# Fixed places for five experts instead of three, with another set of capacities and another order of blocks, in the expert stage of a two-model kernel on one core

## The reference, cut to what matters here

```python
scores = sigmoid(h @ w_router)                       # 256 tokens x 64 experts
idx = top 8 of (scores + router_bias) within the 4 best of 8 groups
gate = scores[idx] / sum(scores[idx]) * 2.5
for each expert e, for the tokens that chose it:
    y = (silu(x @ w_gate[e]) * (x @ w_up[e])) @ w_down[e]     # 1024 -> 256 -> 1024
    out[token] += gate * y
out += (silu(h @ ws_gate) * (h @ ws_up)) @ ws_down            # one shared expert
```

## Time and profile before

| | before |
|---|---|
| median of 3 runs | 1338.97 us (1338.46 to 1340.04) |
| profiled execution, first to last instruction (span) | 1336.3 us |
| what lies around the span (median less span) | 2.7 us |
| PE busy, share of the span | 1311.5 us, 98% |
| DVE, ACT, POOL busy | 52%, 18%, 11% |
| granted PE clock over the core's span | 0.998 of full |
| start of block 0 of the experts | 859.5 us |
| DMA, mean over the span | 269 GB/s |
| DMA, 863 to 1314 us | 420 to 421 GB/s |

### The profile page before, as it was taken

The page is one execution under the profiler, slowest core; times in us unless marked ns, Lnnn a source line. Parts: engine busy times, 40 slices in busy tenths (PEclk is TensorE's granted clock), DMA queues, the critical chain, the costliest instruction groups (busy, mean ns, idle before and its releaser), DMA issues.

```text
span 1336.3 us, 19486 instructions
## 1 busy us (share of the span) xinstructions
PE 1311.5 (98%) x7504; PEld 818.3 (61%) x7504; DVE 694.8 (52%) x1273; ACT 238.2 (18%) x551; POOL 151.4 (11%) x136
## 2 busy tenths in 40 slices
PE   9999999999999999999999999999999999999996
PEld 8667585785789558578577666644444444444433
DVE  1236588877889569877887564322112222222213
ACT  2135321210220341111123152100000000000002
POOL 1125500000011440000003602000000000000001
PEclk9999999999999999999999999999999999999999
DMA  9941155555514428667664414599999999999994
GB/s 380 356 152 34 64 221 200 213 221 216 190 64 166 182 96 330 231 239 301 241 242 155 166 54 168 224 421 421 421 420 414 421 421 421 422 421 421 421 420 195
DMA packets 51072, 359.56 MB, mean 269 GB/s; under 512 B 5920, under 2 KB 6192, under 8 KB 8496
## 3 DMA queue, kind: packets, MB, share of 16 engines
q1 hardware_dynamic: 45312, 324.60, 60.3%
q0 software_dynamic: 5392, 32.05, 6.5%
q10 hardware_dynamic: 288, 1.80, 0.3%
HBM read 356.88 MB, written 1.05 MB: 268 GB/s over the span
## 4 chain that ended last, share of the span: by engine, by line
PE 89%; DVE 8%; issue 1%; DMA 1%; ACT 0%; DVEq 0%; ACTq 0%; SPq 0%
PE ps L1602 14%; PE ps L1076 13%; PE ps L1067 10%; PE ps L1631 7%; PE ps L1527 7%; PE ps L1580 7%; PE ps L843 4%; PE ps L1357 4%; PE ps L1024 4%; PE ps L926 2%; PE ps L1006 2%; PE ps L1350 2%; PE ps L947 2%; DVE ring L2461 1%; PE ps L882 1%
## 5 line engine op out<-in xcount | busy, mean ns | idle before, releaser
L2997 DVE TENSOR_TENSOR masked_and_probs<-ps,gate_rows 128x512 f32<-128x512 f32 x52 | 33.5, 686 | 152.4 <-PE ps L1631 152.4
L1580 PE MATMUL ps<-masked_and_probs,probT 128*128 128x512 f32 x208 | 94.4, 594 | 1.0 <-DVE masked_and_probs L2997 1.0
L1527 PE MATMUL ps<-masked_and_probs,mix_rows 128*128 128x256 f32 (+1 forms) x416 | 93.0, 377 | 0.0
L1527 PEld LDWEIGHTS ps<-masked_and_probs,mix_rows 128*128 128x128 f32 x416 | 75.1, 190 | 28.7 <-issue 19.6
L1067 PEld LDWEIGHTS ps<-xT,ring 128*128 128x128 f32 x768 | 87.7, 192 | 5.0 <-issue 5.0
L1067 PE MATMUL ps<-xT,ring 128*128 128x128 f32 x768 | 88.8, 275 | 0.8 <-issue 0.8
L1076 PE MATMUL ps<-ring,qk_tiles 128*128 128x512 f32 x192 | 85.2, 593 | 0.0
L2985 DVE TENSOR_TENSOR masked_and_probs<-masked_and_probs,ps 128x256 f32<-128x256 f32 x26 | 11.0, 421 | 141.9 <-ACT masked_and_probs L2085 141.9
L1739 ACT ACTIVATE qk_tiles<-ps 128x512 f32<-128x512 f32 (+7 forms) x58 | 30.1, 521 | 245.8 <-PE ps L1067 237.8
L1602 PE MATMUL ps<-ring,vec_rows 128*32 128x512 f32 (+2 forms) x296 | 72.0, 592 | 0.0
L2085 ACT ACTIVATE masked_and_probs<-ps 128x256 f32<-128x256 f32 x26 | 10.0, 383 | 348.2 <-PE ps L1602 348.2
(11 more groups left out here) (525 smaller groups left out, 2512.1 us busy)
## 6 DMA issues: line engine op xcount, KB each, us to landing
ring<-in_stream SPq DMA_DIRECT2D x200, 1024.0 KB, 10.0
qk_tiles<-in_stream SPq DMA_DIRECT2D x46, 1024.0 KB, 20.3
v_rows<-in_ada POOLq DMA_DIRECT2D x12, 1024.0 KB, 5.3
qk_tiles<-in_ada POOLq DMA_DIRECT2D x12, 1024.0 KB, 5.1
vec_rows<-in_stream SPq DMA_DIRECT2D x12, 1024.0 KB, 17.6
con<-in_stream SPq DMA_DIRECT2D x12, 1024.0 KB, 18.7
y_rows<-in_stream SPq DMA_DIRECT2D x12, 1024.0 KB, 20.5
par<-in_stream SPq DMA_DIRECT2D x12, 1024.0 KB, 20.8
```

Of the source, the lines that this page charges most:

```text
L1527: mm = pe.matmul(ps[:, 5 + kk // 2, kk % 2 * 2 * P:kk % 2 * 2 * P + width], h2[:, t, k * P:(k + 1) * P], select[:, t, 0:width], start=t == ...
L1580: mm = pe.matmul(ps[:, q, :], probT[:, buf, 256 + q // 2 * P:256 + (q // 2 + 1) * P], yslot[:, q % 2 * 512:(q % 2 + 1) * 512], start=False ...
L2997: dve.tensor_tensor(yslot[:, cols], ps[:, 5 + half, :], gaterow[:, 1, cols], ALU.mult).then_inc(ready, 1)
```

## The change

`FIXED` goes from 3 to 5, so that experts 3 and 4 also have places of 96 rows. Four of the 64-row places go (21 to 17) and two of 32 rows come (32 to 34): still 61 places, still 25 blocks and 183 chunks. The string of blocks is another one; it has five F blocks (at 0, 1, 2, 4 and 6) instead of three (0, 1 and 3), eight P instead of ten, and the same numbers of Q, M, T and S.

```diff
-FIXED = 3
+FIXED = 5
 UNIT = 32
 PER_MORE = P // UNIT
-WIDTHS = ((3 * P // 4, FIXED), (P, 2), (3 * P // 4, 3), (P // 2, 21), (P // 4, 32))
+WIDTHS = ((3 * P // 4, FIXED), (P, 2), (3 * P // 4, 3), (P // 2, 17), (P // 4, 34))
...
-BLOCKS = "FFQFQPMSMQTPQPPSPPQPPQPPM"
+BLOCKS = "FFFQFPFMQMQPMQPPPSTQPSPQP"
```

## The result

| | before | after |
|---|---|---|
| median (lowest to highest) | 1338.97 us (1338.46 to 1340.04), 5 runs | 1346.95 us (1344.24 to 1348.27), 5 runs |
| ratio of after to before, 95% interval | | 1.0053 [1.0042, 1.0063] |
| profiled execution: time, span | span 1336.3 us | 1348.27 us, span 1346.4 us |

By the ratio the change costs 7.1 us (5.6 to 8.4); the two medians are 8.0 us apart. The forecast was 2.4 us, and its range ended at 1343.6, so it was too low. The profiled execution is the longest of the five runs: its difference of 10.1 us in span has to be read as one execution's.

A forecast was written before the change was run, and what follows sets the result against it. PE was taken as the bound, with the stream of weights only 0.5 us ahead of it at the end. Terms: 0 from PE, 0 from the head start, +2.4 us from the last chunk: 1338.97 + 2.4 = 1341.4 us, range 1338.7 to 1343.6.

The forecast's parts named there:

- PE's work and the places: Expert blocks and loop: two P becoming two F leave PE's sum unchanged, one loop pass; 0, with 0.3 us either way.
- The head start: Before the schedule: fifteen chunks issued instead of nine, 15 us less to move afterwards, but PE waits for no chunk; 0.
- The holes: After the schedule, 850 to 912 us: full slots leave DMA idle; chunks 17, 33 and 69 land 4.9 us after issue.
- The queue runs dry at the start of block 8 and the last chunk is late: Chunk 69 waits for use 52, goes at 1004.1 us; chunk 73 lands 2.8 us later than before, chunk 194 at 1321.1.
- +2.4 us from the last chunk: Loop's down: chunk 194 lands at 1321.1 us, PE wants it at 1318.8, so down starts 2.4 us late.
- chunk 190: Second half of the loop's gate_up: lands at 1311.1 us, wanted at 1312.0, so still in time.
- Block 14, the tightest on the way, by under 2 us: Expert stage, on the way to the loop: block 14's weights still in time, with a margin under 2 us.
- The stall on top of the late end: Rival, block 0: chunk 16 or 17 late, PE waits there on top of 2.4 us; 1342 to 1345 us, chance 0.26.
- second hole: Within the stall rival: idle DMA after 1004 us would add a wait as a block 0 stall does; no separate size.
- faster: Rival, first expert blocks: about 2 us of waits for VectorE dissolve while the early stream keeps its lead; near 1336, chance 0.07.
- No cost: Rival, end of the loop: transfer hidden anyway, last chunk 2 us earlier than counted; 1338.5 to 1339.9 us, chance 0.20.
- an estimate by the 435 GB/s: Weight stream: 2.41 us for a chunk, last landing near 1310 us, the change would cost nothing.

The follow-up runs named there:

- e3: Changed kernel with the kernel before's number of chunks block for block and nine loads ahead of the schedule instead of 15: 1340.06 us, ratio 1.0001.
- e1: Changed kernel with only the first three of its five fixed experts loaded ahead of the schedule (9 loads instead of 15): 1346.67 us, ratio 1.0041.
- e6: Kernel before, nine loads ahead, with its blocks reordered to the changed kernel's number of chunks block for block: 1345.45 us, ratio 1.0039.
- e4: Changed kernel without the loads of the last four chunks (down weights of the loop's pass): 1341.35 us, ratio 1.0010.
- e9: Changed kernel with 28 more transposes just ahead of the loop's wait for its down weights, to keep PE busy: 1343.71 us, ratio 1.0031.
- e2: Changed kernel, still 15 loads ahead, with the kernel before's number of chunks block for block: 1345.45 us, ratio 1.0035.

## Why the prediction was wrong in size, point by point

**PE's work and the places: right.** Two P for two F cost nothing, the loop runs once, and e3 (1.0001) shows it for all that the change does beside order and early loads.

**The head start is worth nothing: right.** e1 and the changed kernel are equal within their intervals.

**The holes: right.** 15 loads are issued ahead of the schedule, and chunks 17, 33 and 69 landed 4.8, 4.8 and 5.1 us after their issue, against 4.9 forecast.

**The queue runs dry at the start of block 8 and the last chunk is late: right in place and mechanism.** Chunk 69 landed 5.1 us after its issue, there. One sentence of the prediction on it is wrong: the blocks 0 to 7 of the kernel before have 6, 6, 12, 6, 12, 6, 6 and 3 = 57 chunks, not 54. The difference of three is the cause in plain words. The changed order has used three chunks fewer when block 8 begins, the 17 slots are full, the DMA engines must idle, and what was not loaded then has to be loaded later, when they are busy all the time. e6 shows it with the order alone (5.2 us), and e3 with the old pattern (nothing). The number was taken from the landing of chunk 73 in both kernels and did not use the false count.

**"+2.4 us from the last chunk": the step that failed.** It is the only term of the sum, and without the last four chunks the changed kernel is 5.6 us faster (e4). It was too small in two ways.

*The lateness.* I had PE start the last `down` 2.4 us late. In the profile it waited 1.0 us for chunk 190, which I had in time by 0.9, and then 3.1 us for chunk 194: 4.1 us. That is not this execution's alone: the same two waits come to 3.7 us in e1 and 3.8 in e6. The last landing was forecast at 1321.1, with block 0 at 859.5; moved by the 3.6 us of this execution that is 1324.7, and it came at 1327.1. Of the 2.4 us, 1.3 arise right behind the restart (chunk 73 landed at 1023.9 instead of 1019.0 + 3.6 = 1022.6, since chunk 70 landed 3.6 us behind chunk 69 and not 2.5). The other 1.1 are pace: (1327.1 - 1023.9) / 121 = 2.506 us for a chunk instead of 2.497, which the prediction had put among its bounds and left out of the sum.

*The clock.* The sum took `down` at 3.69 us behind the wait, with no term for the clock. It took 5.38, with a granted clock of 0.57, 0.50 and 0.81 in three stretches of it, and 5.43 us in e1; in e6 it took 3.73. So this term is 1.7 us in some executions and nothing in others.

**"Block 14, the tightest on the way, by under 2 us":** it was 0.4 us late, one of the prediction's own signs of being wrong, by the same lateness.

Lateness at the end 4.1, block 14 0.4 and clock 1.7 make 6.2 us. The profile has 10.1 - 3.6 = 6.5 to explain, and the runs 5.6 to 8.4.

**The rivals.** The stall on top of the late end had the right sign, but its 1342 to 1345 us are still too low, and its place was wrong: block 0's gate_up took 7.16 us instead of 7.00, no more. It was close: chunk 16 took 6.7 us to land, over the 6.4 that the prediction named, and landed at 866.5 us, just as the second half of block 0 wanted it. The slower restart behind 1004 us is nearer to what this rival named as a second hole. For "faster" one reading was wrong: of the 2 us of waits for VectorE in the earlier trace rows, only 0.9 lie at the start of the experts, the other 1.0 behind the loop's `down`. "No cost" and "faster" are excluded. The prediction also has an estimate by the 435 GB/s that the Trainium skill gives as the ceiling of the fabric ("DMA: Bandwidth & Descriptors", section "Bandwidth"), by which the change would cost nothing. It is excluded too, since the stream ran at 418 GB/s from 1003.8 to 1314 us and the last chunk was late.

**Open.** Why the clock falls behind the wait in some executions only, whether the transposes of e9 gain more than that one `down`, and why the landing that block 0 follows takes 9.6 to 12.2 us.

## What to carry to other kernels

With a fixed number of buffers, a head start is kept only as far as the consumer empties them: count at each step what has been used up, not only what has been loaded. When two bounds are nearly equal, the order of light and heavy items decides. Here the order with the heavy blocks earlier did better (e3 against e1), but not with so many buffers held that an early heavy block lacks them (e2). A wait of PE is not priced by its length alone; what follows it may run at the lower clock. And a profile of one execution can differ from the next by 3.7 us in a part that nobody touched (e9 and the changed kernel), half of the effect itself, so a difference is first looked for in the runs.

## What the runs showed of the hardware

Behind a wait of 3.1 us in which PE stood idle, the granted clock went to 0.50 (1.2 GHz) from 1328 to 1330 us in the changed kernel; with the waits of 3.0 us (e1) and 3.7 us (e2), 1.6 to 1.7 us were lost in each of the three. In e6 it stayed at 1.00 behind a wait of 3.0 us. In e9, with transposes in place of the idle time, it stayed at 1.00 in the one profile. It also fell to 0.50 from 126 to 129 us in the changed kernel, behind waits of 0.9 us at most, and not there in the kernel before. A load of 1 MiB into an empty queue landed 4.7 to 5.1 us after its issue (chunks 15, 17, 33 and 69), and the one behind it, when the queue had just run dry, 3.6 us later instead of 2.5 (chunks 69 and 70 of the changed kernel).
